# Two transformer blocks on one core: conditioning products, delta-rule steps and sigmoid gates in another order

## The reference

```python
# first block, hybrid mixer
u = h @ w_in                                  # three mixers' inputs
y_a = b_gate * conv(c_gate * x_in)            # short convolution: conv 0, 1, 2
y_g = gated_deltanet_mixer(...)               # q, k, v by conv + silu, l2_norm(q), l2_norm(k)
#   m = (k*beta) k^T * decay;  t_inv = inverse of (1 + lower(m)), chunks of 64
y_n = nsa_mixer(...)                          # attention over compressed, chosen and windowed keys
branches = einsum('bsrc,rcd->bsrd', [y_a, y_n, y_g], w_branch)
gates = sigmoid(h @ w_gate + b_gate)
merged = sum(gates * branches);  x = x + merged @ w_out
# then a mixture of 32 experts
# second block, two layers i = 0, 1
mod = silu(c) @ ada_w[i] + ada_b[i]           # 1024 x 6144, c is one row
sh1, sc1, g1, sh2, sc2, g2 = split(mod, 6)
h = rmsnorm(x) * (1 + sc1) + sh1;  x = x + g1 * mixer(h)   # i=0: MLA attention, i=1: Mamba-2
h = rmsnorm(x) * (1 + sc2) + sh2;  x = x + g2 * ff(h)      # i=0: SwiGLU, i=1: 8 experts
```

## Time and profile before

| | us |
|---|---|
| median of 3 runs (lowest, highest) | 2274.25 (2273.01, 2276.13) |
| the profiled execution, its own time | 2275.07 |
| its span | 2273.4 |
| busy: PE, DVE, ACT | 1931.8, 1073.3, 866.5 |
| mean granted clock of PE | 0.949 |

### The profile page before, as it was taken

One profiled execution on the slowest core, in us unless ns is written; L12 is line 12 of the kernel. 1 busy time (PEld: TensorE's weight loads), 2 busy tenths in 40 slices (PEclk: granted clock), 3 DMA queues, 4 the chain that ended last, 5 costly groups with the idle time before them and its releaser, 6 DMA issues.

```text
span 2273.4 us, 30477 instructions
## 1 busy us (share of the span) xinstructions
PE 1931.8 (85%) x12171; PEld 1374.3 (60%) x12171; DVE 1073.3 (47%) x1652; ACT 866.5 (38%) x1196; POOL 46.1 (2%) x115
## 2 busy tenths in 40 slices
PE   7879988996666556698999997999989999999997
PEld 7767767762111111357899897877665674665672
DVE  4653646431211010233555476876474573574572
ACT  4633255210000000234444357765363463463460
POOL 1000200000000000000000000000000000000000
PEclk9999999998888888899999999999999999999999
DMA  7454752579999999859455544446799999999996
GB/s 258 147 205 169 260 204 75 222 308 410 409 409 409 409 409 409 317 177 369 153 180 182 201 131 144 158 143 216 285 393 384 402 408 409 409 407 409 398 408 273
DMA packets 232013, 663.14 MB, mean 292 GB/s; under 512 B 24580, under 2 KB 33320, under 8 KB 231604
## 3 DMA queue, kind: packets, MB, share of 16 engines
q1 hardware_dynamic: 224108, 652.94, 75.3%
q10 hardware_dynamic: 7752, 8.11, 1.3%
HBM read 659.90 MB, written 1.10 MB: 291 GB/s over the span
## 4 chain that ended last, share of the span: by engine, by line
PE 55%; DMA 23%; DVE 11%; ACT 7%; issue 3%; POOL 0%; ACTq 0%; SPq 0%; DVEq 0%; POOLq 0%
PE psum L263 12%; PE psum L265 12%; PE psum L264 12%; PE psum L252 6%; DMA ring<-in_w_expert_down 6%; DMA ring<-in_w_expert_up 5%; DMA ring<-in_w_expert_gate 5%; PE psum L2728 4%; DMA ring<-in_moe_w_gate 3%; ACT w_hi L192 2%; DVE w_lo L202 2%; PE psum L3024 2%; PE psum L2782 2%; PE psum L1323 1%; DMA ring<-in_ada_w 1%
## 5 line engine op out<-in xcount | busy, mean ns | idle before, releaser
L202 DVE TENSOR_TENSOR w_lo<-ring,w_hi 128x1024 fp32r<-128x1024 f32 (+1 forms) x492 | 574.6, 1186 | 433.3 <-ACT w_hi L192 425.5
L192 ACT CAST w_hi<-ring 128x1024 fp32r<-128x1024 f32 (+1 forms) x492 | 497.1, 1020 | 396.2 <-PE psum L265 288.2
L3024 PE MATMUL psum<-ring,hT 128*32 128x512 f32 x960 | 147.7, 747 | 113.5 <-DMA ring<-in_w_expert_gate 62.6
L3024 PEld LDWEIGHTS psum<-ring,hT 128*32 128x32 f32 x960 | 30.3, 124 | 225.6 <-issue 97.5
L263 PE MATMUL psum<-w_hi,xg_hi 128*128 128x512 f32 (+1 forms) x384 | 147.8, 385 | 18.8 <-DVE w_lo L202 18.8
L2728 PE MATMUL psum<-ring,xg_pair 128*64 128x512 f32 (+1 forms) x768 | 155.7, 559 | 4.4 <-DMA ring<-in_moe_w_up 4.4
L2631 DVE TENSOR_TENSOR x<-x,psum 128x1024 f32<-128x1024 f32 x26 | 31.2, 1219 | 253.1 <-PE psum L252 253.1
L264 PE MATMUL psum<-w_hi,xg_lo 128*128 128x512 f32 (+1 forms) x384 | 146.0, 380 | 0.0
L265 PE MATMUL psum<-w_lo,xg_hi 128*128 128x512 f32 (+1 forms) x384 | 145.8, 380 | 0.0
L2728 PEld LDWEIGHTS psum<-ring,xg_pair 128*64 128x64 f32 x768 | 54.1, 137 | 100.7 <-issue 96.7
L3046 PE MATMUL psum<-ring,midT 128*32 128x512 f32 x480 | 70.4, 717 | 44.3 <-DMA ring<-in_w_expert_down 43.9
(11 more groups left out here) (722 smaller groups left out, 3687.5 us busy)
## 6 DMA issues: line engine op xcount, KB each, us to landing
ring<-in_moe_w_down SPq DMA_DIRECT2D x176, 512.0 KB, 11.8
ring<-in_w_expert_gate SPq DMA_DIRECT2D x32, 2048.0 KB, 16.9
ring<-in_moe_w_up SPq DMA_DIRECT2D x128, 512.0 KB, 11.5
ring<-in_moe_w_gate SPq DMA_DIRECT2D x122, 512.0 KB, 12.0
ring<-in_w_expert_down SPq DMA_DIRECT2D x30, 2048.0 KB, 18.1
ring<-in_w_expert_up SPq DMA_DIRECT2D x28, 2048.0 KB, 17.8
ring<-in_ada_w SPq DMA_DIRECT2D x24, 2048.0 KB, 13.1
ring<-in_moe_w_gate SPq DMA_DIRECT2D x64, 384.0 KB, 12.0
```

The costliest lines, as they stand in the source:

```text
L192: a.copy(self.buffers(n, src.shape)[0], src).then_inc(*self.hi_made.up())
L202: v.tensor_tensor(lo, src, hi.bitcast(F32), SUB).then_inc(*self.lo_made.up())
L3024: ins = p.matmul(ps[slots_of(j), g * 512:(g + 1) * 512], M.xg[:, 2 * q + k, slots_of(j)], w[:, j, k, :], start=2 * q + k == 0, stop=2 * q ...
```

## The change

Six things change in the code.

1. **Mix and gdn.** The first pair (0, 0) moves from behind conv 2 to between conv 1 and conv 2 in the ring, and on PE from step 23 to step 17. The pair (0, 1) comes ahead of the first gate unit, on PE at step 24 in place of gdn's level 1; only (0, 2) stays behind it, ahead of the branch unit. The logarithm of the norms goes from step 16 to 15 and the exponentials of the decays get a step of their own; the keys go from step 19 to 18, the turned L from 23 to 20, and DVE's steps follow.
2. **Gates.** Sigmoid(x) becomes Tanh(x/2), and the merge uses (tanh + 1)·branch. The sum is then twice as large, and the last addition to x multiplies by 0.5.
3. **NSA's attention on ACT.** The merge's gate and cast stand behind the copy of the turned probabilities (`after=`) and no longer ahead of it (`beside=`).
4. **`ada_row`** has two halves, used in turn.
5. **Pairs of layer 1.** (1, 1), (1, 2), (1, 3) go to steps 5, 7, 8 of the MLA attention, (1, 4) to the head of ffn, (1, 5) to that of ssm, each with 8 constant products behind it in place of 24. The ring's order follows.
6. **ssm on ACT.** The gate row is written after head 9 and read after head 13, no longer around the norm. The copies of x1's product stand ahead of the first `decays_act`.

```diff
@@ ring, mixer
-    for n, c0 in enumerate((0, 512, 1024)):
-        columns_unit(("conv", n), w_in, c0, 512, feature_parts())
+    for n in range(2):
+        columns_unit(("conv", n), w_in, 512 * n, 512, feature_parts())
+    ada_units(0, 0, 1)
+    columns_unit(("conv", 2), w_in, 1024, 512, feature_parts())
...
-    ada_units(0, 0, 1)
     columns_unit(("gdn", 3), w_in, O_GZ, 512, feature_parts())
+    ada_units(0, 1, 2)
     gate_unit(0, 0)
-    ada_units(0, 1, 3)
+    ada_units(0, 2, 3)
     branch_unit(0, 0)
@@ ring, second block
-        if c == 0:
-            ada_units(1, 1, 2)
-    ada_units(1, 2, ADA_PAIRS)
+    ada_units(1, 1, 4)
     for half in range(2):
         mla_out_unit(half)
+    ada_units(1, 4, 5)
...
+    ada_units(1, 5, ADA_PAIRS)
     for name, g in (("b", 0), ("c", 0), ("x", 0), ("x", 1), ("z", 0), ...
@@ def mix_beside_pe(p, i):
-        if i == 19:
+        if i == 17:
+            ada_pe(p, 0, 0)
+        if i == 18:
             keys_pe(p)
+        if i == 20:
+            decayed_turned_pe(p)
         if i == 21:
+            ada_turn_pe(p, 0, 0)
             values_turned_pe(p)
-        if i == 23:
-            decayed_turned_pe(p)
-            ada_pe(p, 0, 0)
+        if i == 24:
+            ada_pe(p, 0, 1)
@@ def mix_beside_dve(v, i):
+        if i == 17:
+            scaled_dve(v)
         if i == 18:
-            scaled_dve(v)
+            masked_dve(v)
+            weighed_dve(v)
         if i == 19:
-            masked_dve(v)
+            shown_decays_dve(v)
         if i == 20:
-            weighed_dve(v)
+            first_inverse_dve(v)
@@ def gate_act(a, r, half):
-        a.activation(sg[:, :, :], halves_of(banks.of("unit", u)), ACT.Sigmoid).then_inc(*st.act.up("sg", r, half))
+        a.activation(sg[:, :, :], halves_of(banks.of("unit", u)), ACT.Tanh, scale=0.5).then_inc(*st.act.up("sg", r, half))
@@ def merge_dve(v, r, half):
-            settle(v, v.tensor_tensor(sg[:, :, :], sg[:, :, :], branch, MUL), d)
+            settle(v, v.scalar_tensor_tensor(sg[:, :, :], sg[:, :, :], 1.0, branch, ADD, MUL), d)
@@ def mla_beside_pe(p, n):
         if n == 5:
             heads_pe(p, 3)
+            ada_pe(p, 1, 1)
...
+        if n == 7:
+            ada_pe(p, 1, 2)
+        if n == 8:
+            ada_turn_pe(p, 1, 2)
             ada_pe(p, 1, 3)
@@ def ffn_pe(p):
-        norm_pe(p, st, xn_ff, 24)
+        ada_pe(p, 1, 4)
+        norm_pe(p, st, xn_ff, 8)
@@ ssm on ACT
-        a.wait_ge(*st.dve.of("gains"))
-        gates_write_act(a, 1)
         norm_turned_act(a, st, h_ssm, modulated_gain(0), modulated_shift(0))
+        ada_act(a, 1, 5)
...
         x_upad_act(a, 1, 0)
+        split.make_hi(a, split.end(x1) + 3)
+        x_upad_act(a, 1, 2)
+        split.make_hi(a, split.end(x1) + PARTS)
         decays_act(a, 0)
         decays_act(a, 1)
-        split.make_hi(a, split.end(x1) + PARTS)
-        x_upad_act(a, 1, 2)
```

More of the change, by code:

```diff
@@ L1198, in mix_beside_act @@
             banks.empty(st.act, "unit", u)
+            norm_logs_act(a)
         if i == 16:
             roots_act(a)
+        if i == 17:
+            decays_exp_act(a)
+        if i == 18:
+            ada_act(a, 0, 0)
         if i == 19:
@@ L1331, in ada_act @@
         a.wait_ge(*st.pe.of("ada", layer, n))
-        if n:
-            a.wait_ge(*st.pe.of("ada_turned", layer, n - 1))
-        a.copy(ada_row[:, 0:256], banks.of("ada", layer, n)[:, 0:256]).then_inc(*st.act.up("ada", layer, n))
+        if n >= 2:
+            a.wait_ge(*st.pe.of("ada_turned", layer, n - 2))
+        elif layer:
+            a.wait_ge(*st.pe.of("ada_turned", 0, ADA_PAIRS - 2 + n))
+        a.copy(ada_row[:, 256 * (n % 2):256 * (n % 2) + 256], banks.of("ada", layer, n)[:, 0:256]).then_inc(*st.act.up("ada", layer, n))
         banks.empty(st.act, "ada", layer, n)
@@ L1341, in ada_turn_pe @@
         for f in range(2):
-            ins = product(p, ps[:, 4 * f:4 * f + 4], [(ada_row[:, f * P:(f + 1) * P], ident[:, 0:P:32])])
+            ins = product(p, ps[:, 4 * f:4 * f + 4], [(ada_row[:, 256 * (n % 2) + f * P:256 * (n % 2) + (f + 1) * P], ident[:, 0:P:32])])
         ins.then_inc(*st.pe.up("ada_turned", layer, n))
@@ L1431, in merge_dve @@
         if r == 0:
-            v.tensor_tensor(dst, sg[:, :, :], branch, MUL).then_inc(*d.up("merged", r, half))
+            v.scalar_tensor_tensor(dst, sg[:, :, :], 1.0, branch, ADD, MUL).then_inc(*d.up("merged", r, half))
             banks.empty(d, "unit", u)
         else:
-            settle(v, v.tensor_tensor(sg[:, :, :], sg[:, :, :], branch, MUL), d)
+            settle(v, v.scalar_tensor_tensor(sg[:, :, :], sg[:, :, :], 1.0, branch, ADD, MUL), d)
             banks.empty(d, "unit", u)
@@ L1607, in roots_act @@
             banks.empty(e, "norms", half)
+    def roots_act(a):
+        e = S["gdn"].act
         for half in range(2):
@@ L1610, in roots_act, with decays_exp_act @@
             a.activation(rs[:, 4 * half:4 * half + 4, :], rs[:, 4 * half:4 * half + 4, :], ACT.Exp, scale=-0.5).then_inc(*e.up("rs", half))
+    def decays_exp_act(a):
+        st = S["gdn"]
+        e = st.act
         a.wait_ge(*st.dve.of("eg"))
@@ L1900, in attention_pe, with attention_act @@
                     constant_products(p, ps[:, 512:1024], ident, 5)
-    def attention_act(a, st, s, pT, mx, den, scale, jobs, beside=None):
+    def attention_act(a, st, s, pT, mx, den, scale, jobs, beside=None, after=None):
         for n in range(len(jobs) + AHEAD):
@@ L2273, in proj_dve @@
             v.wait_ge(*split.multiplied(u))
-            v.tensor_tensor(dst, dst, halves_of(banks.of("unit", u)), ADD).then_inc(*st.dve.up("x"))
+            v.scalar_tensor_tensor(dst, halves_of(banks.of("unit", u)), 0.5, dst, MUL, ADD).then_inc(*st.dve.up("x"))
             banks.empty(st.dve, "unit", u)
@@ L3251, in modulation_gains_dve @@
         d = st.dve
-        settle(v, v.tensor_tensor(mod[:, :], mod_all[:, 48 * layer:48 * layer + 48], colrange("ada_b_2", 48 * layer, 48 * layer + 48), ADD), d)
+        n = 40 if layer else 48
+        settle(v, v.tensor_tensor(mod[:, 0:n], mod_all[:, 48 * layer:48 * layer + n], colrange("ada_b_2", 48 * layer, 48 * layer + n), ADD), d)
         for s_ in range(2):
@@ L3415, in mla_beside_dve @@
             rope_queries_dve(v, 1)
[L3416 to L3417 removed]
+        if n in (6, 8):
+            ada_turn_dve(v, 1, n // 2 - 2)
         if n == 9:
[L3419 removed]
+            ada_turn_dve(v, 1, 3)
         if n == 9:
@@ L3729, in ssm_pe @@
         e = st.pe
-        norm_pe(p, st, xn_ssm, 24)
+        ada_pe(p, 1, 5)
+        norm_pe(p, st, xn_ssm, 8)
         ps = banks.take(p, "dt")
@@ L3921, in ssm_act @@
                 split.make_hi(a, ssm_part(g, hh) + PARTS)
+                if h == 9:
+                    a.wait_ge(*st.dve.of("last_gate"))
+                    gates_write_act(a, 1)
+                if h == 13:
+                    gates_load_act(a, 1)
                 if hh == 0 and g in (1, 2):
@@ L4064, in ssm_dve @@
         split.make_lo(v, split.end(b) + PARTS)
+        ada_turn_dve(v, 1, 5)
+        v.wait_ge(*S["ada"].dve.last())
+        v.tensor_tensor(mod[:, 40:48], mod_all[:, 88:96], colrange("ada_b_2", 88, 96), ADD).then_inc(*d.up("last_gate"))
         v.wait_ge(*st.pe.of("daT"))
```

66 lines of the change are left out of this document (27 added, 39 removed).

## The result

The changed kernel takes **2246.84 us** (median of 4 runs, 2243.68 to 2249.49), the kernel before 2275.19 (4 runs, 2273.01 to 2279.87). The ratio is 0.987, 95% interval 0.9857 to 0.9882, so 28.4 us less. The prediction was 2246.5.

The account below looks back on a forecast made before the run. PE was taken as the bound, busy 85% of the span, with stalls and slow clock in the dense stages; terms -16.3, -1.0, -7.5, +0.9 and -4.3 sum to -28.2, giving 2246.5 us, range 2235 to 2262.

Parts of the forecast that it names:

- Mix and gdn: Dense stages of layer 0: net 16.3 us less, from stalls removed minus new waits.
- taken out: Mix and gdn: PE stalls, slow keys, late branch weights and level 2's slow step go, 24.05 us in all.
- put in: Mix and gdn: bank waits 3.7 and 1.9, slower clock 1.7, turned values' wait for ACT 0.5; 7.8 us together.
- Attention: NSA's attention with tanh gates and the copy moved: net 1.0 us less, between 5 less and 3 more.
- The two halves: NSA's attention: shorter stalls at the copy win 6.6 us; the copy in the job chain costs 5.6 us.
- MLA: MLA: two of five pairs leave, with one weight wait and two turned rows, against new copy waits; 7.5 us less.
- the heads of ffn and ssm: Heads of ffn and ssm: pairs replace constant products for free, but the two turns cost 0.9 us.
- ssm: ssm: z0's 5.60 us stall falls to about 1, x0's silu wait costs 2.3; net 4.3 us less.
- Not half the gain: Rival, 18%: new bank waits drop the clock and the tail hangs on DVE; mix and gdn give 8 us, 2254.8.
- Not every table load: Rival, 10%: ACT's chain paces attention, so every load removed counts; 8 us more gain, 2238.5.
- Not slower: Rival, 5%: PE stands still in all twelve attention jobs and the clock stays at 1.2 GHz; 2288 us.
- Not the same: Rival, 4%: the ring's intake bounds the time and late loads are late elsewhere; 2274 us.

Follow-up runs that it names:

- v1: The whole change, but gdn 3's product takes the pair of banks that ACT's copy of the turned L frees; 2241.73 us against 2275.33 for the kernel before.
- v2: v1 with other bank pairs for the turned L and values and the first pair's turn a step later; 2239.58 us, ratio 0.9834 to the kernel before.
- e_tanh: Only the gates by tanh, with the merge's factor, on the kernel before; 2271.64 us against 2277.40.
- e_full_latecopy: The whole change, but with the copies of x1's product back behind the decays; 2246.68 us, ratio 0.9873 to the kernel before.
- e_ssm: Only the copies of x1's product moved ahead of the first heads' decays in ssm, on the kernel before; 2273.47 us against 2275.33.
- e_tanh_after: Gates by tanh plus the copy of turned probabilities ahead of the merge's gate and cast, on the kernel before; 2275.93 us, ratio 0.9991.
- e_mix: Only layer 0's ring order and the steps of mix and gdn, on the kernel before; 2258.18 us against 2277.40.
- e_pairs: Only the move of layer 1's pairs, with the gate row's new places, on the kernel before; 2266.38 us against 2277.40.
- again: The whole change run once more, unchanged (the second execution), against the kernel before; 2246.79 us, ratio 0.9867.
- v2_beside: v2 with the merge's gate and cast again ahead of the copy of the turned probabilities on ACT; 2237.10 us against 2277.03 for the kernel before.

## Why the prediction was right

**Mix and gdn, 16.3 said, 15.8 and 15.1 measured.** Everything taken out went as the sum had it (7.22, 0.92, 2.17, 2.4, 8.74, 2.6); the cast that waited 15.4 us for the branch weights no longer does. Of what was put in, the bank wait ahead of part 24 was 3.96 where 3.7 stood, the one ahead of the turned L 2.23 where 1.9 stood, q and k were in time. Too small was the clock behind them: 1.7 was taken, and part 24 alone lost 2.6 and the part behind the turned L 1.6 (5.25 us to the first pair's turn, where v1 has 3.64). Left out was a gain of the same size: level 1's wait for Z fell from 2.52 to 1.42, and its step ran at 1.00. v1 and v2 show that what was put in was not needed.

**Attention, 1.0 said, 0.7 and 1.1 measured.** The two halves have the right signs and nearly cancel, as the sum had it, but their sizes of 6.6 and 5.6 are not shown: e_tanh won 4.6 without the copy in front, and the copy gave 4.1 back. Since kernels that leave attention alone are 0.5 to 0.6 shorter in it too, the net is at most 0.6 us, and may be nothing. The prediction counted seven table loads, 9.0 us; the trace has lost eight, 10.3 us, which changes nothing in the sum, as it goes by the stalls. The pace of a job was expected at 7.3 and is 7.69, since the copies of the later jobs are the long ones (0.90).

**The stretch ahead of attention** was not in the sum: 1.6 us by a low clock, which is granted in some executions and not in others (last section).

**MLA, 7.5 said, 7.1 measured**, and the heads of ffn and ssm cost 0.2 and not 0.9; the turned rows there are nearly hidden.

**ssm, 4.3 said, 3.1 measured (1.4 in the second execution).** The stall fell to 0.8 as said, and PE waits 2.2 for x0's silu where 2.3 stood. What failed here is the reason given: "Now DVE frees its banks, and the copy is early". The first half alone does it. DVE frees them because of the bank rotation, which the parts in mix and gdn had moved, and e_full_latecopy shows that in this kernel the copy could have stayed. On the kernel before, the copy's place takes the stall away (e_ssm, 5.6 to 0.7), and the times show 3.0 us for it, with an interval from 0 to 6.

**The rivals.** Not half the gain: mix and gdn gave 15.8 where that rival had 8, and the tail did not hang on DVE's convolutions, since v1, with the wait gone, wins all of it behind gdn. Not every table load: e_tanh's attention is 4.6 shorter for 10.3 us of loads. Not slower: PE did begin to wait in more jobs, and the clock in that stretch was hardly lower (it was 0.93 and 0.90 in the first two thirds of attention before, 0.94 and 0.88 in e_tanh_after); the new waits were mostly of 0.4 to 1.5 us. Not the same: the 28.4 us are far clear of the noise, and in mix and gdn no wait for a load above 2 us has taken the place of the one for the branch weights.

The parts agree with the whole as far as the noise lets one see: 18.9 (e_mix) + 2.0 (e_tanh_after) + 9.3 (e_pairs) are 30.2, and e_ssm's 3.0 would make 33.2, against 28.4 to 30.3 for the whole. Each part is uncertain by some 3 us. ssm's stall, which e_mix and e_ssm each take away and which can go only once, is a reason for the larger sum, but the times can't show it.

**Luck.** That the median lies 0.3 us from the forecast is luck. The four executions span 5.8 us, and the terms missed by -0.5, -1.6, -0.3, -0.2, -0.4, +0.7, -1.2 and +1.0 us, so the profile gained 25.6 where the sum had 28.2.

The Trainium skill (ScalarE: Activation LUTs, What ACT_TABLE_LOAD costs) has 2.66 us for a switch, half of it a drain. In e_tanh the gate starts within 0.1 us of the exp's end, and in the earlier trace rows the load started at the exp's end and the gate at the load's end. So the load's figure agrees, and a drain of 1.38 us is not seen at this switch. With such a drain the eight switches that are gone would, as an estimate from that figure, be 21.3 us of ACT, and ACT is 10.7 less busy.

## What to carry to other kernels

When a rotation hands out buffers, look at who frees the buffer that the next user takes, not only at the order of the work: naming one other pair of banks (v1) took away a wait of 4.0 us and 2.6 us of slow products behind it. Its time is not clear of the change's; with further pairs named (v2) the stretch is 10.6 us shorter. Look further down too, since the same edits changed who frees a pair in ssm. Price a stall with the clock behind it, since the work that follows at the low clock cost 1.6 us more behind a wait of 2.2 us, and 2.6 behind one of 4.0. When two edits are bundled, time each alone; here tanh won 5.5 us (3.0 to 8.0) and the new order beside it gave most of that back.

## What the runs showed of the hardware

Between the compression and its last tiles PE stands still for 2.55 us, in every kernel. In some executions it comes back at full clock and the first turned tile takes 0.33 us, in others at half, and it takes 0.47 with the sixteen behind it at 3.3 us where they took 1.9. First again, then v2, then v2_beside:

```profile
274.28 0.47 PE L1015 MATMUL psum<-ident,nsa_s 128*128 128x128 f32 x1 [2.55 <-DVE nsa_s L2208]
274.55 3.33 PE L1015 MATMUL psum<-ident,q 128*64 128x128 f32 x16
```

```profile
263.69 0.47 PE L1015 MATMUL psum<-ident,nsa_s 128*128 128x128 f32 x1 [2.54 <-DVE nsa_s L2209]
263.96 3.21 PE L1015 MATMUL psum<-ident,q 128*64 128x128 f32 x16
```

```profile
261.70 0.33 PE L1015 MATMUL psum<-ident,nsa_s 128*128 128x128 f32 x1 [2.55 <-DVE nsa_s L2207]
```

All five kernels with the mix of before had 0.33, four with the new mix 0.47, v1 and v2_beside 0.33 and v2 0.47, though v2 and v2_beside are the same program up to there. So the length of the stall does not settle it; what does is open. It is worth 1.4 to 1.6 us each time, and it is why a landmark can jump by that much without any instruction having moved. The 2.23 us wait ahead of the turned L shows the same: four executions went on at a granted clock of 0.58 to 0.64, and v1, with the same instructions up to there, at 1.00, which is worth 1.6 us.
